# A 128-slot and a 64-slot expert interleaved block by block, and second projections read as two neighbouring rows per partition

## The reference

```python
def moe_swiglu(x, router, w_in, w_out):
    logits = (xt @ router).astype(jnp.float32)
    top_v, top_i = lax.top_k(logits, MOE_TOP_K)
    top_w = jax.nn.softmax(top_v, axis=-1)
    gates = jnp.sum(jax.nn.one_hot(top_i, N_EXPERTS, dtype=jnp.float32) * top_w[..., None], axis=1)
    for e in range(N_EXPERTS):
        out = out + gates[:, e:e + 1].astype(x.dtype) * swiglu(xt, w_in[e], w_out[e])
```

## Time and profile before

| | us |
|---|---|
| median of 3 runs | 1451.48 (1450.18 to 1451.59) |
| profiled execution, its own time | 1448.69 |
| span of the profile, first to last instruction | 1447.0 |
| PE busy (matmul) | 1397.1 (97%) |
| DVE busy | 1135.3 (78%) |
| ACT busy | 962.1 (66%) |

### The profile page before, as it was taken

The page is one execution under the profiler, slowest core; times in us unless marked ns, Lnnn a source line. Parts: engine busy times, 40 slices in busy tenths (PEclk is TensorE's granted clock), DMA queues, the critical chain, the costliest instruction groups (busy, mean ns, idle before and its releaser), DMA issues.

```text
span 1447.0 us, 18516 instructions
## 1 busy us (share of the span) xinstructions
PE 1397.1 (97%) x7394; PEld 1183.1 (82%) x7394; DVE 1135.3 (78%) x789; ACT 962.1 (66%) x804; POOL 54.6 (4%) x66
## 2 busy tenths in 40 slices
PE   9999999999999999999999999999999999999996
PEld 9987779999989887887778887777887877888774
DVE  5456655444566589889999888999889999889997
ACT  5344544433445467778987777997777897777895
POOL 1001200000000013000002000001000000000000
PEclk9999999999999999999999999999999999999998
DMA  9654646555555359999999999999999999999993
GB/s 360 223 174 146 204 156 222 186 192 175 182 197 175 117 206 365 361 359 359 414 420 420 390 355 357 378 420 421 410 354 367 362 417 421 417 366 348 405 415 140
DMA packets 158743, 446.89 MB, mean 309 GB/s; under 512 B 7088, under 2 KB 46000, under 8 KB 158656
## 3 DMA queue, kind: packets, MB, share of 16 engines
q1 hardware_dynamic: 156832, 439.38, 81.3%
q0 software_dynamic: 1824, 6.33, 1.3%
HBM read 444.63 MB, written 1.05 MB: 308 GB/s over the span
## 4 chain that ended last, share of the span: by engine, by line
PE 67%; DVE 27%; ACT 3%; issue 2%; POOL 0%; DVEq 0%; ACTq 0%; POOLq 0%
PE ps L1422 19%; PE ps L1424 19%; PE ps L1423 19%; DVE wlo L964 17%; DVE wlo_more L964 5%; PE ps L1840 2%; PE ps L1841 2%; ACT whi L834 1%; PE ps L1877 1%; PE ps L1759 1%; PE ps L1834 1%; DVE h L1323 1%; DVE y_lo L964 1%; DVE wlo L387 1%; DVE gT_small L964 1%
## 5 line engine op out<-in xcount | busy, mean ns | idle before, releaser
L964 DVE TENSOR_TENSOR wlo<-raw,whi 128x2048 fp32r<-128x2048 f32 (+1 forms) x214 | 479.3, 2259 | 49.0 <-ACT whi L834 48.4
L834 ACT ACTIVATE whi<-raw 128x2048 fp32r<-128x2048 f32 x208 | 396.9, 1917 | 88.8 <-PE ps L1424 78.3
L387 DVE TENSOR_TENSOR wlo<-raw,whi 128x2048 fp32r<-128x2048 f32 x80 | 183.6, 2295 | 155.3 <-ACT whi L380 155.3
L380 ACT ACTIVATE whi<-raw 128x2048 fp32r<-128x2048 f32 x82 | 156.8, 1912 | 153.2 <-PE ps L1424 150.0
L1422 PE MATMUL ps<-xT_hi,whi 128*128 128x256 f32 x576 | 163.3, 284 | 0.0
L1424 PE MATMUL ps<-xT_hi,wlo 128*128 128x256 f32 x576 | 163.0, 283 | 0.0
L1423 PE MATMUL ps<-xT_lo,whi 128*128 128x256 f32 x576 | 163.0, 283 | 0.0
L1840 PE MATMUL ps<-whi,xg_small 128*128 128x512 f32 x336 | 133.0, 396 | 3.8 <-DVE wlo L964 3.1
L1422 PE MATMUL ps<-whi,xg_big 128*128 128x512 f32 x336 | 133.3, 397 | 0.6 <-DVE wlo L964 0.6
L1424 PE MATMUL ps<-whi,xg_big 128*128 128x512 f32 x336 | 131.1, 390 | 0.0
L1841 PE MATMUL ps<-wlo,xg_small 128*128 128x512 f32 x336 | 131.0, 390 | 0.0
(11 more groups left out here) (253 smaller groups left out, 2695.2 us busy)
## 6 DMA issues: line engine op xcount, KB each, us to landing
raw<-in_moe_w_in SPq DMA_DIRECT2D x168, 1024.0 KB, 7.4
raw<-in_moe_w_out SPq DMA_DIRECT2D x84, 1024.0 KB, 8.0
more_raw<-in_moe_w_in SPq DMA_DIRECT2D x56, 1024.0 KB, 7.0
more_raw<-in_moe_w_out SPq DMA_DIRECT2D x28, 1024.0 KB, 9.0
raw<-in_ret_w_in SPq DMA_DIRECT2D x23, 1024.0 KB, 6.7
raw<-in_ffn_w_in SPq DMA_DIRECT2D x22, 1024.0 KB, 4.9
raw<-in_ffn_w_out SPq DMA_DIRECT2D x11, 1024.0 KB, 4.8
raw<-in_ret_w_out SPq DMA_DIRECT2D x8, 1024.0 KB, 4.9
```

What stands on the lines that cost most here:

```text
L380: nc.scalar.activation(whi[:, u % SPLIT, :], src, ACT.Copy).then_inc(hi_done, 1)
L387: nc.vector.tensor_tensor(wlo[:, u % SPLIT, :], src, whi[:, u % SPLIT, :].bitcast(F32), ALU.subtract).then_inc(lo_done, 1)
L834: nc.scalar.activation(moe_split(n)[0], moe_raw(n), ACT.Copy).then_inc(hi_done, 1)
L964: return nc.vector.tensor_tensor(dst, src, hi.bitcast(F32), ALU.subtract)
```

## The change

1. The two hand-written orders become one list `STREAM` of 336 units. Job j (big) and job j+1 (small) alternate by block: the big one's gate of block b, its second projection of block b-1, its up of block b, and then the same three of the small one. A job's last second projection falls into the first block of the next pair. The sides' work (silu, product, turn, split, gather, scatter) is placed relative to the ends of the parts in this list.
2. To let two jobs run together, big and small sums have PSUM banks 4, 5 and 6, 7; turns use banks 2 and 3, gathers bank 1; `y_hi`, `y_lo`, `selT` and `xg_small` exist twice; `hid4`, `up_rows`, `gate_rows` share the memory of `act4`.
3. The second projection is read with two neighbouring rows per partition (8 KB in one run) where it was two rows 128 apart (4 KB each). So the chunks of the hidden layer that PE turns are every second column (`hidden_chunk`).
4. The first small gather is a step of its own after unit 5; in the first job weighing and placing of the gates and `see_excess` come later.

```diff
-    SMALL_STREAM = [(part, b, q) for part, b in (("gate", 0), ("up", 0), ("gate", 1), ("up", 1), ("out", 0), ("gate", 2),
...
-    GATHER = {i: k for k, i in enumerate((13, 15, 17, 19, 25, 27, 29, 31))}
+    for phase in range(JOBS * (LAST + 1)):
+        pair, b, j = phase // (2 * (LAST + 1)), phase // 2 % (LAST + 1), 2 * (phase // (2 * (LAST + 1))) + phase % 2
+        START[j, b] = len(STREAM)
+        if phase == JOBS * (LAST + 1) - 1:
+            STREAM += units_of(j, "gate", b) + units_of(j, "up", b) + units_of(j - 1, "out", b)
+            STREAM += units_of(j, "out", b - 1) + units_of(j, "out", b)
+        else:
+            before_out = [] if j < 2 and b == 0 else units_of(j, "out", b - 1) if b else units_of(j - 2, "out", LAST)
+            STREAM += units_of(j, "gate", b) + before_out + units_of(j, "up", b)
+    END = {(j, part, b): n for n, (j, part, b, q) in enumerate(STREAM)}
...
+    SILU_AT = {END[j, "gate", b] + half: (j, b, half) for j, b, half in BIG_HALVES}
+    MUL_AT = {END[j, "up", b] + half: (j, b, half) for j, b, half in BIG_HALVES}
+    TURN_AT = {END[j, "up", b] + 1 + 2 * half: (j, b, half) for j, b, half in BIG_HALVES}
+    LO_AT = {END[j, "up", b] + 2 + 2 * half: (j, b, half) for j, b, half in BIG_HALVES}
+    GATE_AT = {END[j, "gate", b]: (j, b) for j, b in SMALL_BLOCKS}
+    GATE_TURN_AT = {END[j, "gate", b] + 2: (j, b) for j, b in SMALL_BLOCKS}
+    UP_AT = {END[j, "up", b]: (j, b) for j, b in SMALL_BLOCKS}
+    UP_TURN_AT = {END[j, "up", b] + 1: (j, b) for j, b in SMALL_BLOCKS}
...
+    GATHER_AT = {START[j, b] + i: (pair, k) for pair in range(1, JOBS // 2)
+                 for k, (j, b, i) in enumerate([(2 * pair - 2, 1, 6), (2 * pair - 2, 1, 8), (2 * pair - 2, 1, 10),
+                                                (2 * pair - 1, 1, 6), (2 * pair - 1, 1, 8), (2 * pair - 1, 1, 10),
+                                                (2 * pair - 2, 2, 6), (2 * pair - 2, 2, 8)])}
+    SEL_AT = {START[j - j % 2, 2] + 5 + 2 * (j % 2): j for j in range(JOBS)}
+    Y_AT = {END[j, "out", LAST]: j for j in range(JOBS - 1)}
+    SCATTER_AT = {END[j, "out", LAST] + (4 + 4 * t if j < JOBS - 2 else 2 + 3 * t): (j, t) for j in range(JOBS - 1) for t in range(T)}
...
-    moe_out = moe_w_out.rearrange("a e (k p) n -> p (a e k) n", p=P)
+    moe_out = moe_w_out.rearrange("a e (u p c) n -> p (a e u) (c n)", p=P, c=2)
...
-                return moe_out[:, bass.ds(e * (EFF // P) + 8 * b + 2 * q, 2), :], 2
+                return moe_out[:, bass.ds(e * (EFF // P // 2) + 4 * b + q, 1), :], 1
...
+            for n in range(MOE_UNITS):
+                copy_rows(n)
+                moe_hi(n + MSPLIT)
+                big_drains(n)
+                small_drains(n)
+                if n in SEL_AT:
+                    copy_selT(SEL_AT[n], 3)
...
+                if n in GATHER_AT:
+                    copy_gathered(*GATHER_AT[n])
...
+            def hidden_chunk(rows, c):
+                pair = rows[:, c // 2 * 2 * P:(c // 2 + 1) * 2 * P]
+                return pair.rearrange("p (n c) -> p c n", c=2)[:, c % 2, :]
...
+                if q == 0 and part == "up" and blocks(j, b) > 1:
+                    pe.wait_ge(small_mul, blocks(j, b) - 1)
+                    pe.wait_ge(up_copied, 7 * (j // 2) + 2 * b)
+                    if b == 2:
+                        pe.wait_ge(selT_ready, j + 2)
...
+                if n in TURN_AT:
+                    j, b, half = TURN_AT[n]
+                    pe.wait_ge(big_mul, 7 * (j // 2) + 2 * b + half + 1)
+                    hidden_turn(half, turn_bank(j, b, half))
...
+                if q == 0 and part == "up":
+                    pe.wait_ge(big_lo, halves(j, b))
```

More of the change, by code:

```diff
@@ L91, in build, with units_of @@
-    assert len(GATHER) == KD
+    def units_of(j, part, b):
+        return [(j, part, b, q) for q in range(BLOCK_UNITS[b])]
+    LAST = len(BLOCK_UNITS) - 1
+    STREAM, START = [], {}
+    for phase in range(JOBS * (LAST + 1)):
[7 more added lines that the diff above has]
+            STREAM += units_of(j, "gate", b) + before_out + units_of(j, "up", b)
@@ L494, in _, with moe_unit @@
                 load_unit(sp, U_ATT_OUT + i, 0, att_out[:, 2 * i:2 * i + 2, :], 2)
-            def moe_unit(u, i, e, slot, dst, free, small=False):
-                src, rows = moe_source(i, e, small)
+            def moe_unit(part, b, q, e, slot, dst, free):
+                src, rows = moe_source(part, b, q, e)
                 sp.wait_ge(lo_done, free)
@@ new lines, in copy_first_small, with copy_gathered @@
+            def copy_first_small():
+                for g in range(2):
+                    act.wait_ge(gathered, g + 1)
+                    nc.scalar.activation(xg_small[0][:, 4 * g:4 * g + 4, :], bank(6 + g, 4),
+                                         ACT.Copy).then_inc(small_copied, 1)
+            def copy_gathered(pair, k):
+                src = ps[:, 1, 0:2 * (P + HALF)].rearrange("p (s n) -> p s n", s=2)
+                act.wait_ge(gathered, gathers(pair) + k + 1)
+                nc.scalar.activation(xg_big[pair % 2][:, k, :, :], src[:, :, 0:P], ACT.Copy).then_inc(big_copied, 1)
+                nc.scalar.activation(xg_small[pair % 2][:, k, :].rearrange("p (s n) -> p s n", s=2), src[:, :, P:P + HALF],
@@ L1761, in gather_step, with gather_first_small @@
                 return last
[L1763 to L1773 removed]
+            def gather_first_small():
+                pe.wait_ge(sel_second, T)
+                for k in range(KD):
+                    last = gather_step(k, ps[:, 6 + k // 4, k % 4 * P:(k % 4 + 1) * P], sel[:, 0, :, P:2 * P], HALF)
+                    if k % 4 == 3:
+                        last.then_inc(gathered, 1)
@@ new lines, in hidden_turn, with big_unit @@
+            def hidden_turn(half, at):
+                for k in range(4):
+                    last = pe.transpose(ps[:, at, k * P:(k + 1) * P],
+                                        hidden_chunk(act4, 4 * half + k), ident[:, :])
+                last.then_inc(big_turned, 1)
+            def big_unit(n):
+                j, part, b, q = STREAM[n]
+                if q == 0 and part == "gate":
+                    if b == 0 and j > 0:
+                        pe.wait_ge(big_copied, KD * (j // 2))
+                    if blocks(j, b) > 1:
+                        pe.wait_ge(small_silu, blocks(j, b) - 1)
+                        pe.wait_ge(gate_copied, 7 * (j // 2) + 2 * b)
+                    if gathered_by(START[j, b]):
+                        pe.wait_ge(small_copied, gathered_by(START[j, b]))
+                if q == 0 and part == "up" and blocks(j, b) > 1:
[3 more added lines that the diff above has]
+                        pe.wait_ge(selT_ready, j + 2)
+                if part == "out" and q % 2 == 0:
+                    pe.wait_ge(big_lo, 7 * (j // 2) + 2 * b + q // 2 + 1)
+                    if b == 0 and q == 0 and j > 0:
+                        pe.wait_ge(summed, T * (j - 1))
+                pe.wait_ge(lo_done, U_MOE + n + 1)
+                big_product(part, b, q, xg_big[j // 2 % 2], *moe_split(n))
@@ L1951, in _ @@
                     for t in range(T):
-                        scatter(t)
+                        scatter(t, selT[1], y_hi[1], y_lo[1], 6)
                         pe.wait_ge(summed, T * (JOBS - 1) + t + 1 + T * p)
@@ L1968, in _ @@
             for t in range(T):
-                scatter(t, 6 * (1 - t))
+                scatter(t, selT[1], y_hi[1], y_lo[1], 6 * (1 - t))
 _INS = ['x', 'ln_g', 'ln_b', 'ret_w_in', 'ret_gn_g', 'ret_gn_b', 'ret_w_out', 'kv_w', 'moba_w_q', 'moba_w_out',
```

578 lines of the change are left out of this document (286 added, 292 removed).

## The result

The changed kernel takes 1456.63 us, median of 7 runs (1454.12 to 1457.3). The kernel before takes 1451.48, median of its 7 runs beside them (1449.41 to 1455.84). The ratio is 1.0037 (1.0026 to 1.0049): 0.37% **slower**, where 1439.0 was forecast. The profiled execution has a span of 1453.5 us, 6.5 more than before.

A forecast was written before the change was run, and what follows sets the result against it. Big jobs were taken as bound by PE, small ones by DVE. Idle of 10.5 + 2 x 7.5 + 12.4 = 37.9 us for 50.3 saves 12.4: 1451.5 - 12.4 = 1439 us, range 1414 to 1462.

The forecast's parts named there:

- 37.9 us idle, for 50.3 before: 12.4 us less: Expert stage: PE's idle after the change, summed over four pairs, set against stage minus priced work before; saves 12.4 us.
- The walk: PE waits at block boundaries, stepped through with trace durations: 10.5 us, twice 7.5, and 12.4 for the four pairs.
- Work of PE, 853 us: Whole expert stage: passes at 0.2275 us plus turns, gathers, scatters and selection make 853 us of PE work.
- Small jobs bound by DVE: In the old order's small jobs, DVE's 100.8 us sum sets the length, against 90.5 of PE work.
- The product: At block 2's first turn, now 1.82 us after the up unit, DVE's product ends at 2.35; part of 1.6 idle.
- `selT`: In block 2 the big up waits for ACT's copy of the small job's selection: 2.3 us per pair.
- First pair's `big_lo`: Pair 1's small up waits for `big_lo`, second half done at 12.9 while PE is there at 8.8: 4.2 us.
- slower, block boundaries: Rival: PE meets a closed ring at 31 block boundaries, 102 us or 84 (1485 us); chance 0.13, most under 1465.
- the second, that idle time only moves: Rival: idle moves from small jobs to 31 block boundaries at 1.5 to 1.7 us each; 1449 to 1454; chance 0.12.
- Lower clock, forecast as gone: Profile after was to show no clock dips; before, jobs 4 and 6 held a few microseconds at 1.2 GHz.
- Strided loads taken as nothing: `hidden_chunk` turns loading every second float cost nothing; upper bound 60.7 us, kept as a rival at 1500, chance 0.07.
- Reads: Stage reads near 395 GB/s flat, their floor of 841 us below PE's 853; slower-reads rival 1521 us, chance 0.01.

The follow-up runs named there:

- e7_before_half_lo: Kernel before, with DVE computing only the first half of each low part in the expert stage; 1418.12 us, ratio 0.9766.
- e2_rows_apart: Changed kernel with the second projection read as before, two rows 128 apart, so turns load contiguous chunks; 1451.75 us, ratio 1.0004.
- e1_sel_early: Changed kernel with the two selection transposes of each pair two units earlier in block 2; 1443.31 us, ratio 0.9953.
- e3_filled_wait: Changed kernel with PE multiplying `ident` by itself eight times into an unused bank during the `selT` wait; 1452.75 us, ratio 1.0015.
- e9_two_mends: Changed kernel with earlier selection transposes and the first pair's small up waiting only for the product; 1435.98 us, ratio 0.9903.
- e10_three_mends_again: Changed kernel with earlier selection transposes, rows read as before, and the first pair's small up waiting only for the product, measured again; 1433.61 us, ratio 0.9885.
- e5_three_mends: Changed kernel with earlier selection transposes, rows read as before, and the first pair's small up waiting only for the product; 1437.83 us, ratio 0.9900.

## Why the prediction was wrong

**The step that failed** is the subtraction "37.9 us idle, for 50.3 before: 12.4 us less". The 37.9 were waits, walked through one by one; the 50.3 were stage minus work at the price of quiet passes. Waits were 34.6 us before and 35.8 after. The walk put everything else between priced work and stage at nothing, and the subtraction so counted it as saved: it was 16.5 us before and 21.4 after. Held like against like the walk says +3.3, a slightly slower kernel, and the waits did grow by 1.2. Two terms that the sum had at nothing make the rest: the turns and what stands around them (+4.3) and passes at the lower clock (+3.5), less 2.9 of other passes. Together 1.2 + 4.3 + 3.5 - 2.9 = 6.1, the growth of the stage.

**Work of PE, 853 us: right as a sum of prices.** Of what e7_before_half_lo has above it only about 5 us are neither waits, nor right behind one, nor the lower clock. (The 0.2275 of a pass is the 0.91 us over the four passes from 875.79 to 876.70 in the earlier trace rows; the three passes that the prediction names are 0.68 us, or 0.2267 each, which would make the work 2.7 us less.)

**Small jobs bound by DVE: right.** Halving its low parts shortens the old order by 31 us, and every wait that the trace of before names is one for DVE.

**Waits of the boundaries.** The product: 2.38 us behind the slot against 2.35 in the walk; 4.9 us at 10 places. `selT`: 9.3 us at 4 places, 2.3 each in the walk. First pair's `big_lo`: 3.9 for 4.2. The last pair's waits for `gT_lo` and `y_lo` came as well (6.3 - 3.9 = 2.4 and 2.1). `xg_small` cost 0.4 at three places for 1.3 in the walk. No wait stands at a place that the walk does not have, and PE met no closed ring at each block: 9.3 of the 35.8 us stand at four places, and the rest is small. So the mechanism of the rival "slower, block boundaries" did not come, though 1456.63 lies among the times at which it had most of its chance. The rival closest to what came is the second, that idle time only moves, though its times (1449 to 1454) end below the one measured.

**Lower clock, forecast as gone ("no clock dips"): wrong.** It was read from the earlier trace rows that long waits of PE are followed by it, but the walk's own waits of 2.3 and 4.2 us were priced without it. Behind them stand four of the five stretches of the changed kernel's stage, at 1.6 us each; the fifth, behind the first small gather, no part of the prediction has.

**Strided loads taken as nothing: wrong, in the direction of its bound, at a fourteenth of it** (4.3 of 60.7 us). The Trainium skill (SBUF — State Buffer, Door 1: The DMA port swizzle) gives full bandwidth to two successive accesses within a line of 16 bytes; the traces do not agree for the loads of the big turns, at 207 ns for 139, and nearly agree for those of the small ones, at 196 for 192.

**Reads: right.** The stage moves 380 GB/s and peaks at 424; ACT, which waited for data 2.0 us in its largest row before, names no such wait after. Packets fell from 158,743 to 144,408 with no gain to be seen (e2_rows_apart, with the old packets, is faster). "Near 395 flat" was too smooth for a kernel that waits at its ends.

**Before unit 8, `experts_sorted`: nothing, as forecast.** The reads do stop: 0 GB/s in 528 to 533 and 10 in 533 to 538, for 374 and 369 before. But they are back at 368 in 538 to 543, and no wait of ACT or PE for data stands there.

What stays open: why a load of 128 strided columns costs 68 ns in one kind of turn and 4 in the other, and why the clock fell behind only some of equal waits: behind three of four of 2.3 us here, at two of four of 2.9 in the kernel before (at 889.42 and 1118.11), and behind the wait of 2.4 us in the last pair in e1_sel_early and e3_filled_wait but not in e9_two_mends. Untested is also the stretch behind the first small gather.

The version to keep is that of e10_three_mends_again: 1433.61 us, 1.15% below the kernel before (0.96% to 1.34%), and 1.6% below the median of the change as given; e5_three_mends, the same kernel, has 1437.83 and 1.0%.

## What to carry to other kernels

Compare waits with waits. Stage minus ideal work also holds the long first passes behind waits and side work and the stretches at the lower clock. Whoever walks through a new order and counts its waits must hold them against the waits that the trace of the old one shows, or price the rest for the new one too. And price each new wait of the busiest engine of over 2 us with a stretch at the lower clock that may stand behind it, here 1.6 us, behind three of four waits of 2.3 and behind the one of 3.9; often moving one copy or one condition by a unit takes it away.

## What was not expected of the hardware

- PE's clock fell to the lower level right behind waits of 2.35 and 3.86 us in the midst of full work, and did not when 8 products of 128 columns stood in the wait of 2.35 us.
- Its clock also fell, at 549.33, right behind 32 products of 64 columns that ran from 545.69 to 549.18 with no wait.
- Passes right behind a turn start 0.31 and 0.24 us apart instead of 0.2275, though nothing is waited for; the one right behind a waited pass starts 0.31 behind it.
- A weight load of every second float of 128 partitions takes 204 to 207 ns where one of adjacent floats takes 139, in one form of matmul, and 196 for 192 in another.
